# Layer 1's modulation vectors in a two-layer state-space, convolution and expert kernel: ten of twelve weight blocks scaled and summed on VectorE in the first layer's gate and up stage

## The reference

```python
def modulate(h, shift, scale):
    return h * (1 + scale) + shift

silu_c = jax.nn.silu(c)[:, None, :]
silu_cc = jax.nn.silu(c_ctx)[None, None, :]
for l in range(DEPTH):
    need_ctx = l < DEPTH - 1
    mod_lat = jnp.split(silu_c @ w_ada[l] + b_ada[l], N_MOD, axis=-1)
    mod_ctx = jnp.split(silu_cc @ w_ada[l] + b_ada[l], N_MOD, axis=-1)
    a_lat = modulate(rmsnorm(h_lat, g_pre_mix[l]), mod_lat[0], mod_lat[1])
    a_ctx = modulate(rmsnorm(h_ctx, g_pre_mix[l]), mod_ctx[0], mod_ctx[1])
    ...                                   # mixer, y_lat and y_ctx
    h_lat = h_lat + mod_lat[2] * rmsnorm(y_lat, g_post_mix[l])
    f_lat = modulate(rmsnorm(h_lat, g_pre_ffn[l]), mod_lat[3], mod_lat[4])
    h_lat = h_lat + mod_lat[5] * rmsnorm(ffn(f_lat), g_post_ffn[l])
```

## Time and profile before

| | before |
|---|---|
| median of 3 runs | 1668.63 us (1667.31 to 1669.69) |
| the profiled execution, its own time | 1667.8 us |
| its span | 1666.1 us |
| TensorE busy (matmul) | 1591.3 us, 96% |
| VectorE busy | 703.0 us, 42% |
| ScalarE busy | 375.8 us, 23% |
| mean granted TensorE clock | 0.991 of full |
| gate and up stage of layer 0 | about 331 to 624 us |
| down stage of layer 0 | about 624 to 763 us |
| layer 1's mixer | about 763 to 978 us |
| experts | about 978 us to the end |

### The profile page before, as it was taken

One profiled execution on the slowest core, in us unless ns is written; L12 is line 12 of the kernel. 1 busy time (PEld: TensorE's weight loads), 2 busy tenths in 40 slices (PEclk: granted clock), 3 DMA queues, 4 the chain that ended last, 5 costly groups with the idle time before them and its releaser, 6 DMA issues.

```text
span 1666.1 us, 26910 instructions
## 1 busy us (share of the span) xinstructions
PE 1591.3 (96%) x11354; PEld 963.6 (58%) x11354; DVE 703.0 (42%) x1657; ACT 375.8 (23%) x841; POOL 80.5 (5%) x156
## 2 busy tenths in 40 slices
PE   6999999989999999999898999899999999999997
PEld 3655456868888888885676545334344443334344
DVE  4987983574544456877589360000010001000101
ACT  4333543321111010015756522100000000000002
POOL 2210100000000003000003100000000000000000
PEclk9999999999999999999999999999999999999999
DMA  8503553235536515204144389999999999999995
GB/s 320 168 8 121 208 147 101 85 116 153 152 108 195 148 42 127 89 3 150 57 125 112 92 344 388 413 415 407 407 412 414 408 405 411 414 409 406 411 412 211
DMA packets 170839, 396.41 MB, mean 238 GB/s; under 512 B 34499, under 2 KB 93483, under 8 KB 153562
## 3 DMA queue, kind: packets, MB, share of 16 engines
q1 hardware_dynamic: 165344, 391.23, 63.6%
q0 software_dynamic: 4112, 3.34, 1.3%
q10 hardware_dynamic: 1258, 0.07, 0.0%
HBM read 389.36 MB, written 1.05 MB: 234 GB/s over the span
## 4 chain that ended last, share of the span: by engine, by line
PE 82%; DMA 8%; DVE 5%; ACT 2%; SPq 1%; issue 1%; ACTq 0%; DVEq 0%
PE ps L1362 80%; DMA arena<-in_moe_w_up_dram 4%; PE ps L1365 2%; DMA arena<-in_moe_w_down_dram 2%; DMA arena<-in_w_in_dram 1%; DMA arena<-in_moe_w_gate_dram 1%; SPq L705 1%; DVE arena L2743 1%; ACT work L866 0%; ACT work L865 0%; DVE work L2418 0%; DVE work L2420 0%; DVE work L2423 0%; DVE norms L2421 0%; DVE norms L2569 0%
## 5 line engine op out<-in xcount | busy, mean ns | idle before, releaser
L1362 PE MATMUL ps<-arena,work 128*32 128x256 f32 (+6 forms) x4572 | 605.5, 480 | 13.9 <-DMA arena<-in_moe_w_up_dram 7.7
L1362 PEld LDWEIGHTS ps<-arena,work 128*32 128x32 f32 (+2 forms) x4572 | 271.4, 125 | 318.4 <-issue 249.3
L1362 PE MATMUL ps<-arena 128*128 128x256 f32 (+2 forms) x1152 | 289.7, 479 | 5.7 <-DMA arena<-in_w_in_dram 4.7
L1362 PEld LDWEIGHTS ps<-arena 128*128 128x128 f32 (+1 forms) x1152 | 185.9, 185 | 99.6 <-issue 72.3
L1362 PE MATMUL ps<-work 128*64 128x64 f32 (+11 forms) x2300 | 222.1, 323 | 12.7 <-DVE work L2991 6.7
L3222 DVE TENSOR_TENSOR work<-work,ps 128x768 f32<-128x768 f32 (+4 forms) x26 | 18.6, 726 | 510.4 <-PE ps L1362 510.4
L1362 PEld LDWEIGHTS ps<-work 128*64 128x64 f32 (+5 forms) x2300 | 156.2, 150 | 71.3 <-issue 53.6
L1362 PE MATMUL ps<-work,arena 128*128 128x256 f32 (+1 forms) x588 | 126.5, 367 | 0.0
L1282 ACT ACTIVATE work<-ps 128x512 f32<-128x512 f32 (+3 forms) x35 | 17.7, 505 | 444.8 <-PE ps L1365 444.8
L1362 PEld LDWEIGHTS ps<-work,arena 128*128 128x128 f32 (+1 forms) x588 | 103.2, 190 | 13.4
L1362 PE MATMUL ps<-apad,dg 64*64 64x512 f32 (+1 forms) x384 | 69.2, 500 | 9.0 <-ACT dg L874 5.9
(11 more groups left out here) (438 smaller groups left out, 1392.8 us busy)
## 6 DMA issues: line engine op xcount, KB each, us to landing
arena<-in_moe_w_down_dram SPq DMA_DIRECT2D x66, 1024.0 KB, 17.2
arena<-in_moe_w_up_dram SPq DMA_DIRECT2D x54, 1024.0 KB, 18.4
arena<-in_w_ada_dram SPq DMA_DIRECT2D x23, 2048.0 KB
arena<-in_moe_w_gate_dram SPq DMA_DIRECT2D x46, 1024.0 KB, 15.8
arena<-in_moe_w_up_dram SPq DMA_DIRECT2D x26, 768.0 KB, 16.9
arena<-in_moe_w_gate_dram SPq DMA_DIRECT2D x22, 768.0 KB, 15.8
norms<-in_moe_w_down_dram SPq DMA_DIRECT2D x13, 1024.0 KB, 16.8
arena<-in_w_in_dram SPq DMA_DIRECT2D x6, 2048.0 KB
```

Source lines behind the costliest of these rows:

```text
L1362: return pe.matmul(o, lhs, rhs, start=start, stop=stop)
```

## The change

All twelve blocks of layer 1 are now loaded around the gate and up stage. Two (blocks 0 and 1 of unit (1,0)) stay on TensorE: `modulation` ahead of the stage as before, and the second right after `added_sum(1)`. The other ten (`SUMMED`) go to VectorE. `weigh` takes a block in pieces of 128x512: the weights times the condition of their row (a scalar for each partition), added to a running sum in SBUF. Blocks 2 and 3 of unit (1,0) serve both streams and take 16 pieces each; those of units (1,1) and (1,2) take 8, for the latents' vector alone. That is 2 x 16 + 8 x 8 = 96 pieces, of which 16 are a plain `tensor_scalar` that starts a sum, and 80 a `scalar_tensor_tensor`. One block is done for each i = 1 to 10, and `parts_` says after which operations of a half its pieces stand. `summed_modulation` on TensorE adds the 128 partitions of a finished sum with a column of ones: 8 matmuls for unit (1,0) in i = 3, 4 matmuls for (1,1) in i = 7, 4 for (1,2) after the first product of the down stage. `modulate(1, 2)` moves from layer 1's mixer to the down stage. A block's slot is now freed by VectorE (`ada_part`), and the order of the ring's steps changes.

```diff
         NU = 2 * D
         BLOCKS = 4
-        SECOND = 5
+        ON_PE = 2
+        SUMMED = {i: (1, 0, ON_PE + i - 1) for i in range(1, 1 + BLOCKS - ON_PE)}
+        UNIT_AT = {1: 1 + BLOCKS - ON_PE, 2: 1 + 2 * BLOCKS - ON_PE}
+        for u in (1, 2):
+            SUMMED.update({UNIT_AT[u] + b: (1, u, b) for b in range(BLOCKS)})
+        streams_of = lambda u: (1,) if u else (0, 1)
+        pieces = lambda i: 8 * len(streams_of(SUMMED[i][1]))
...
+            used.append(("ada_part", summed_before(summed[0] + 1)) if summed else
+                        ("ada_done", BLOCKS * UNITS.index((l, u)) + b + 1))
...
-            else:
-                add_unit(*UNITS[5])
...
             if l == 0:
+                add_unit(*UNITS[3], ON_PE)
                 for i in range(FU):
-                    if i < BLOCKS:
-                        add_block(*UNITS[3], i)
-                    if SECOND <= i < SECOND + BLOCKS:
-                        add_block(*UNITS[4], i - SECOND)
+                    if i - 1 in SUMMED:
+                        add_block(*SUMMED[i - 1])
                     at["ffn", i] = len(steps)
...
+                add_block(*SUMMED[FU - 1])
                 at["down"] = len(steps)
...
+            def summed_modulation(u, bank):
+                blocks = [i for i in SUMMED if SUMMED[i][1] == u]
+                pe.wait_ge(sem("ada_part"), summed_before(blocks[-1] + 1))
+                if u:
+                    pe.wait_ge(sem("mod"), 3 + u)
+                for s in streams_of(u):
+                    v = mod_sum(u, s).rearrange("p a i (m j r) -> p j (a i) m r", j=4, r=32)
+                    for j in range(4):
+                        last = mm(ps[32 * j:32 * j + 32, bank, :], one_at[:, 1 - s:33 - s], v[:, j], u > 0, s == 1)
+                last.then_inc(sem("ada_done"), len(blocks))
...
                     if b == 0:
                         added_sum(1)
+                        modulation(at["ada", 1, 0, 1], 1, 7)
                     pe.wait_ge(sem("ffn_s"), 4 * b + 1)
                     make(b, 5, lambda k: s1[:, k, :], lambda k: T_of(1)[:, k])
+                    if j == 0 and i in UNIT_AT.values():
+                        summed_modulation(SUMMED[i][1] - 1, 7)
...
-                    if j and i < BLOCKS - 1:
-                        modulation(at["ada", 1, 0, i + 1], i + 1, 7)
-                    if j and SECOND <= i + 1 < SECOND + BLOCKS:
...
+                        if p == 0 and g == 0:
+                            summed_modulation(2, 7)
...
-                layer, u, b = AFTER_TURN[l]
-                modulation(at["ada", layer, u, b], b, ADA_BANK[layer, u])
+                if l == 0:
+                    modulation(at["ada", 0, 2, 3], 3, ADA_BANK[0, 2])
...
+                        for x in range(first, last):
+                            k, s, q = x // again, streams_of(u)[x % again // 4], x % 4
+                            o = mod_sum(u, s)[:, q]
+                            w = weights(n)[:, k, 512 * q:512 * q + 512].rearrange("p (i t) -> p i t", i=2)
+                            c_k = sc[:, 2 * blk + k, s:s + 1]
+                            if k == 0 and i in (1, *UNIT_AT.values()):
+                                ts_(o, w, c_k, None, ALU.mult).then_inc(sem("ada_part"), 1)
+                            else:
+                                dve.wait_ge(sem("ada_part"), before_ + x + 1 - again)
+                                stt(o, w, c_k, o, ALU.mult, ALU.add).then_inc(sem("ada_part"), 1)
...
+                            parts_ = ([0, 0, 0, 2, 5, 5], [5, 9, 11, 13, 16, 16])[j] if pieces(i) == 16 else \
+                                ([0, 0, 0, 2, 5, 5], [5, 7, 7, 8, 8, 8])[j]
```

More of the change, by code:

```diff
@@ L348, in hybrid_backbone, with mod_sum @@
         BLOCKS = 4
-        SECOND = 5
+        ON_PE = 2
[5 more added lines that the diff above has]
+        pieces = lambda i: 8 * len(streams_of(SUMMED[i][1]))
+        summed_before = lambda i: sum(pieces(x) for x in SUMMED if x < i)
+        mod_sums = (spare[:, 1152:1152 + NU].rearrange("p (a i t) -> p a i t", a=4, i=2), inner)
+        def mod_sum(u, s):
+            return mod_sums[0 if u == 2 else s]
         steps, used, at = [], [], {}
@@ L355, in add_block @@
                            .rearrange("(k p) n -> p k n", p=P))])
-            used.append(("ada_done", BLOCKS * UNITS.index((l, u)) + b + 1))
+            summed = [i for i in SUMMED if SUMMED[i] == (l, u, b)]
+            used.append(("ada_part", summed_before(summed[0] + 1)) if summed else
+                        ("ada_done", BLOCKS * UNITS.index((l, u)) + b + 1))
         def add_unit(l, u, blocks=BLOCKS):
@@ L2998, in _, with weigh @@
                     tt_(T_of(4), second[0], T_of(2), ALU.subtract).then_inc(sem("ffn_tokens"), 1)
+                    def weigh(i, first, last):
+                        l, u, blk = SUMMED[i]
+                        n, before_ = at["ada", l, u, blk], summed_before(i)
+                        again = pieces(i) // 2
+                        if first == 0:
+                            dve.wait_ge(sem(f"ring_in{n % 3}"), landed[n])
+                            if i == 1:
+                                link(dve.memset(one_at, 0.0))
+                                link(dve.memset(one_at[:, 1:2], 1.0))
+                            if u and blk == 0:
+                                dve.wait_ge(sem("ada_done"), BLOCKS * UNITS.index((l, u)))
+                        for x in range(first, last):
[8 more added lines that the diff above has]
+                                stt(o, w, c_k, o, ALU.mult, ALU.add).then_inc(sem("ada_part"), 1)
                     for b in range(2 * FU):
                         i, j = b // 2, b % 2
+                        parts_ = [0] * 6
+                        if i in SUMMED:
+                            parts_ = ([0, 0, 0, 2, 5, 5], [5, 9, 11, 13, 16, 16])[j] if pieces(i) == 16 else \
+                                ([0, 0, 0, 2, 5, 5], [5, 7, 7, 8, 8, 8])[j]
                         if b + 1 < 2 * FU:
@@ L3007, in _ @@
                             seventh_sums(0, 0)
-                        if b == 2 * BLOCKS:
-                            modulate(1, 0, 7, rowsT)
-                        if b == 2 * (SECOND + BLOCKS):
-                            modulate(1, 1, 7, rowsT)
+                        if j and i in UNIT_AT.values():
+                            modulate(1, SUMMED[i][1] - 1, 7, rowsT)
                         if i and j == 0:
```

27 lines of the change are left out of this document (17 added, 10 removed).

## The result

The changed kernel takes 1672.21 us (median of 22 runs, 1668.19 to 1675.7), the kernel before 1668.68 in the same session (22 runs, 1666.19 to 1670.92): a ratio of 1.0020, 95% interval 1.0013 to 1.0027. It is slower by 3.5 us. The prediction was 1665.2, range 1660.5 to 1671.0, so it was wrong in sign and just outside its range. The profiled execution took 1672.54 us (span 1670.7, mean granted clock 0.988; before 1667.8, 1666.1 and 0.991).

A forecast was written before the change was run, and what follows sets the result against it. TensorE, busy 96% of the span, was taken as the bound in gate and up. The terms -14.35 + 6.3 + 4.25 + 0.4 gave -3.4 us, so 1665.2 us for the median, range 1660.5 to 1671.0.

The forecast's parts named there:

- Blocks gone, -14.35: Gate and up: seven modulation blocks leave TensorE's saturated queue, 2.05 us each, 14.35 us off.
- sums, +4.25: Sums over partitions on TensorE, two in gate and up, one in the down stage: 2.05 and twice 1.1 us.
- The first weights, +6.3: Start of gate and up: ffn 0 loads later, delaying the scaled tokens and everything after by 6.3 us, clock loss included.
- VectorE, 0: Gate and up: the 96 pieces, at 0.67 us each, are covered by TensorE's time; cost 0, range 0 to 2.
- wrong if TensorE waits in i = 3: Gate and up: a TensorE wait in i = 3 was named as one sign that the forecast is wrong.
- the ring: Gate and up: VectorE frees block slots, so the next ffn load hangs on it; claimed to cost nothing.
- rival 1: Gate and up: VectorE becomes the bound in i = 1 and 2, the kernel is slower, 1672.0 us; chance 0.14.
- The down stage, +0.4: Down stage: 1.5 MB more ahead of `B` delays it 4.4 us against 4.2 margin; +0.4 us, range 0 to 2.
- The mixer, 0: Layer 1's mixer: blocks leaving TensorE save nothing, as VectorE, then ScalarE, is the chain; 0, range -6 to 0.
- Rival 2: Layer 1's mixer pays too, its stretch being shared by both engines: up to 1657.8 us; chance 0.08.
- rival 3: Start of gate and up: the late first weights cost nothing, giving 1658.9 us; chance 0.06.
- Everything after shifts by the same amount: After layer 1's mixer: all later work, the experts' loads too, moves by the same amount, with no further cost.

The follow-up runs named there:

- e3: The changed kernel with the loads of `B` for layer 1's scan issued one weight step of the down stage earlier: 1668.66 us.
- e1: The changed kernel with ffn 0, the first gate and up weights, loaded ahead of the second block again: 1663.14 us.
- e2: The kernel before with ffn 0 loaded late, behind blocks 0 and 1 of unit (1,0); the blocks all still on TensorE: 1676.15 us.
- e8: The changed kernel with 80 of the 96 VectorE pieces cut to 16 of 512 columns: 2359.62 us, as tokens were routed differently; read only up to the mixer.
- e4: The kernel before with three of four blocks of unit (1,2) in layer 1's mixer cut to one of 8 matmuls each: 1668.09 us.
- before with the fill: The kernel before with 28 matmuls that compute nothing behind `added_sum(1)`, in TensorE's gap ahead of product 5 of half 0: 1666.52 us.
- e6: The changed kernel with 25 matmuls that compute nothing on TensorE ahead of its wait for ffn 0: 1669.14 us.
- e7: The changed kernel with `added_sum(1)` ahead of products 1 and 2 of half 0 on TensorE, ffn 0 still late: 1667.13 us.
- e5 with the fill: The changed kernel with ffn 0 first, `B` one step earlier, and 18 matmuls that compute nothing ahead of product 5 of half 0: 1656.97 us.

## Why the prediction was wrong

**Blocks gone, -14.35, and sums, +4.25: right.** From product 5 of half 0 to the end of the stage the changed kernel takes 11.05 us less (+7.87 to -3.18); 7 x 2.05 less the two sums in the stage (2.05 and 1.1) is 11.2. The period is 24.17 us without a block and 26.73 in i = 3 (SP wakes at 424.04, 450.77 and 474.94); of that 0.40 is the wait below, and in e3, without it, it is 26.25, where 26.2 was forecast. The third sum is 1.09 (-3.18 to -2.09).

**The first weights, +6.3: right in its mechanism, too small by 1.4 us.** Products 1 and 2 came 6.5 us later than their place in the queue, not 5.9: ffn 0 took 9.4 us from issue to use, for 8.9. ffn 1's loads were issued behind it from 332.15 on, which the lone load of the estimate did not have; no run separates what that costs. The clock's loss there was 2.35 us (6.07 for 3.72), for 1.7. The sum was cheaper by 0.6, the 0.6 of slack was there: 6.5 + 2.35 - 0.6 - 0.6 = 7.65, and 7.66 was measured in the trace (7.87 less the 0.21 ahead). e1 and e2 give 9.1 and 7.2 for it. It was seen as the largest cost and then given its size from a lone load, and with the milder clock.

**VectorE, 0: right,** at 0.66 from start to start. The price was one wait of 0.40 in i = 3 at 429.59, which by the prediction's own sign ("wrong if TensorE waits in i = 3") counts against it. It came with a late load, by the ring that was put at "nothing": ffn 3 went out at 403.12, when VectorE had freed its slot, behind the block's load of 399.87. It was wanted at 414.4 and came at 415.77. In e3, where VectorE doesn't wait for that load, and in the second trace of the changed kernel, where it waits for 1.10 us, TensorE has no such wait. e8 puts all that the pieces cost at 0.47. So rival 1 (1672.0) met the time by chance, and not the cause.

**The down stage, +0.4: the first of two steps that failed.** It cost 2.96 us in the trace (-2.09 to +0.87), and e3, which takes it out, 3.5 in the times. The mechanism was right (`B` comes late, and VectorE's weight sums behind it), and so was the margin of 4.2 us; the delay was mis-sized. The 1.5 MB more ahead of `B` were priced at 340 GB/s, 4.4 us, and delayed it by 7.0. From the end of the stage to the first load of `B` went 2.06 us before (624.38 to 626.44) and 7.69 now, 5.6 more, and from there to VectorE's use of it 1.4 us more. 7.0 less 4.2 is 2.8, and the wait is 2.69. A part of the difference is the rate (315 GB/s from 626.20 on, not 340); how much is SP's own time of issuing stays open. That small DMAs hold SP for long was on the row: the earlier trace rows shows 8.63 us for four.

VectorE's wait for `B` answers to the first line of the earlier trace rows:

```profile
645.36 0.69 DVE L2422 TENSOR_TENSOR arena<-work,cf 128x512 f32<-128x512 f32 x1 [10.18 <-DMA work<-in_ssm_b_im_dram]
```

**The mixer, 0: right,** by e4. The 0.47 that the table shows between 917 and 935 is scatter of the first trace of before. Rival 2 is refuted, and so is rival 3 (by e1 and e2).

**"Everything after shifts by the same amount": the second step that failed.** No term stood for the clock behind waits that the change does not touch. It cost 1.15 us at 815 and 1.63 at 979, 2.8 in all, where the down stage was missed by 2.55. The windows of the second place, changed kernel, columns as in the earlier trace rows:

```profile
978.50:980.50 2.00, 1.11 (x10) 1.04 (x11) 1.24 (x8) 0.00 (x0) 0.00 (x0) 1.00 1.03 412
980.50:982.50 2.00, 2.00 (x13) 2.00 (x12) 1.66 (x10) 0.00 (x0) 0.00 (x0) 0.57 1.02 408
982.50:984.50 2.00, 2.00 (x12) 2.00 (x12) 1.66 (x11) 1.40 (x4) 0.00 (x0) 0.57 1.02 406
```

Before, the same stretch was granted 1.00 throughout:

```profile
977.50:979.50 2.00, 1.11 (x10) 1.04 (x10) 1.34 (x8) 0.00 (x0) 0.00 (x0) 1.00 1.03 410
979.50:981.50 2.00, 2.00 (x20) 2.00 (x20) 1.69 (x10) 0.79 (x3) 0.00 (x0) 1.00 1.03 410
```

Over all traces:

| kernels | x128 at 815, us | router's x32, us |
|---|---|---|
| before, twice; e4; before with the fill | 5.26, 5.33; 5.24; 5.33 | 3.78 in all four |
| changed, twice; e3; e6; e7; e8 | 6.41, 6.34; 6.48; 6.59; 6.57; 6.61 | 5.41 in all six |
| e1; e5; e5 with the fill | 6.02; 5.16; 6.59 | 5.41 in all three |
| e2 | 6.61 | 5.41 |

So at the router this is hardly chance of an execution: the four traces of kernels with the program of before and its loads at the start are fast, the ten others lose 1.6 us. The loads alone do not decide it: e1, e5 and e5 with the fill have the order of before at the start, and are slow. What differs is which of the two levels of the granted clock (1.2 or 2.4 GHz) the records got: it stayed at 1.00 in the four and fell to 0.50 in the ten. The traces show one thing more. In thirteen of them (not in e1) the clock goes to half once already some 9 us ahead of the router, around the end of a wait of 2.36 us. In the four fast traces it falls there 8.3 to 7.5 us ahead of the router's records, in eight of the slow ones 9.4 to 9.2 us (e5: 8.4). Where one fall comes seems to bear on whether there is a next one, but no run tests it. At the scan's product (x128) the ten scatter from 5.16 to 6.61, so there no rule shows.

The Trainium skill, page "TensorE: Matmul & The Clock Gate", section "Part 1: The HAM clock gate", says that the transition point between the two clock levels is run-variable. The two traces of the changed kernel bear it out at product 5 (5.09 and 6.71), the four of the first line do not. What decides the clock at these two places stays open. A shift of 2.2 us alone (before with the fill) does not change it, while e2, which is before but for one load's place, does, in its one trace.

The sum with the sizes found, in the order first weights, down stage, clock, wait in i = 3: -3.4 + 1.4 + 2.55 + 2.8 + 0.4 = +3.75 us, where the medians give 3.5. The two profiled executions differ by 4.7, of which 1.1 to 1.3 is the scatter at the first experts. So of the 6.9 us between forecast and result the clock term and the down stage make 5.35. With the wait of the down stage taken out (e3) the time is 1668.66, inside the range but still not faster than before.

## What to carry to other kernels

When a step is moved in a queue of loads, price all that is issued behind it by what a row shows for such a load with others around it, not for a lone one at the best rate, and ask what stands behind the first waiter on the consumer's queue: here a sum of squares behind two products turned a late load into a late norm. Freed engine time is worth nothing if the loads that paid for it come late, and both could be had: the same change with ffn 0 back in its old place and the loads of `B` one step earlier (e5) is 7.9 us faster than before. Where a wait on TensorE can't be removed, count the work behind it at both clock levels, and give places that the change only shifts a range of their own.

## What the runs showed of the hardware

- SP was busy for 1.96 us with four DMAs of `w_down` (384 KB each, e3) and for 2.02 with four of 512 KB (before), and for 7.64 us with eight (changed): the second four took 5.7. The DMA share was 1.10 over the 9 us from 626.20 on.
- The same four small DMAs of `b_re` (64 KB each) kept SP busy for 7.01 (e3) and 8.63 us (before) behind four DMAs of weights, and for 10.55 (changed) behind eight.
- 32 equal records behind the same wait of 0.89 us took 3.78 us in four traces and 5.41 in ten, with nothing in between, and the granted clock stayed at 1.00 in the four and fell to 0.50 in the ten.
- 80 operations of 128x512 (`scalar_tensor_tensor`) took 0.74 us each, 0.66 from start to start; of 128x16, 0.23 each (e8).
- A fill that left 1.97 us idle did not keep the clock up (0.5 granted between 339 and 341); fills that left 0.43 and 0.61 did (8 records in 1.97 us).
